# One mask a group, a new order in the recurrence with decays, and both ends of the program rewritten, in a two-layer hybrid block

## The reference, cut to what matters

```python
def rmsnorm(x, g):
    xf = x.astype(jnp.float32)
    y = xf * lax.rsqrt(jnp.mean(xf * xf, -1, keepdims=True) + EPS)
    return (y * g).astype(x.dtype)

# in ssd_group, for each group g with its E = 4 heads:
cb = jnp.einsum('bclgn,bcsgn->bgcls', Cm, Bm)              # one matrix a group
y_diag = jnp.einsum('bgecls,bcsgep->bclgep', cb[:, :, None] * jnp.exp(segsum(a_dt)), X)   # four decays a group
...
return rmsnorm(h, final_norm)[:, N_META:]
```

## Time and profile before

| | |
|---|---|
| runs, median (lowest to highest) | 1816.45 us (1816.36 to 1817.53) |
| the profiled execution, its own time | 1813.89 us |
| its span, first to last instruction | 1812.0 us |
| busy: TensorE / VectorE / ScalarE / GpSimd | 1770.1 / 1205.4 / 729.5 / 50.1 us |
| TensorE's mean granted clock | 0.995 of full |

### The profile page before, as it was taken

How to read it: one execution, slowest core, us unless ns; L and a number is a source line. 1 busy time by engine, 2 the same in 40 slices (tenths; PEclk the granted TensorE clock), 3 DMA queues, 4 the chain that set the end, 5 groups by cost and what they waited for, 6 DMA issues and landing times.

```text
span 1812.0 us, 35225 instructions
## 1 busy us (share of the span) xinstructions
PE 1770.1 (98%) x13934; PEld 1685.2 (93%) x13934; DVE 1205.4 (67%) x1702; ACT 729.5 (40%) x1074; POOL 50.1 (3%) x130
## 2 busy tenths in 40 slices
PE   7999999999999999999999999999999999999996
PEld 7988888999999999999999888888889999999996
DVE  7788846446367778874334777777776788888323
ACT  5454431112134233222223777777774322223221
POOL 0221200000000000000000000000000000000000
PEclk9999999999999999999999999999999999999998
DMA  4322232221222222322222212112123222223221
GB/s 154 109 77 86 94 107 61 80 70 58 70 83 92 92 83 91 93 91 95 96 74 81 62 62 62 57 53 61 59 59 93 83 92 93 93 93 99 92 96 62
DMA packets 39936, 149.89 MB, mean 83 GB/s; under 512 B 4384, under 2 KB 5408, under 8 KB 39216
## 3 DMA queue, kind: packets, MB, share of 16 engines
q1 hardware_dynamic: 38672, 142.16, 24.6%
q10 hardware_dynamic: 1184, 6.60, 1.1%
HBM read 146.62 MB, written 2.13 MB: 82 GB/s over the span
## 4 chain that ended last, share of the span: by engine, by line
PE 82%; issue 8%; DVE 6%; ACT 3%; POOL 1%; DMA 0%; DVEq 0%; ACTq 0%; POOLq 0%
PE gp L365 70%; PE small L411 4%; PE small L422 1%; PE small L605 1%; PE small L615 1%; DVE wlo L1112 1%; POOL dec L1734 1%; DVE spb L1563 1%; PE small L464 1%; DVE gr L1152 1%; ACT lbuf L959 1%; ACT lbuf L962 0%; DVE sp_lo L1587 0%; DMA rdec<-in 0%; ACT whi L698 0%
## 5 line engine op out<-in xcount | busy, mean ns | idle before, releaser
L365 PE MATMUL gp<-hn_hi,whi 128*128 128x264 f32 (+1 forms) x3216 | 661.6, 287 | 15.3 <-DVE wlo L1112 11.8
L365 PE MATMUL gp<-hn_hi,wlo 128*128 128x264 f32 (+1 forms) x3216 | 653.4, 285 | 0.0
L365 PE MATMUL gp<-hn_lo,whi 128*128 128x264 f32 (+1 forms) x3216 | 653.2, 284 | 0.0
L698 ACT ACTIVATE whi<-raw 128x1024 fp32r<-128x1024 f32 (+1 forms) x249 | 273.6, 1099 | 796.0 <-PE gp L365 785.9
L1112 DVE TENSOR_TENSOR wlo<-raw,whi 128x1024 fp32r<-128x1024 f32 (+1 forms) x249 | 317.5, 1275 | 345.6 <-ACT whi L698 337.5
L365 PEld LDWEIGHTS gp<-hn_hi,whi 128*128 128x128 f32 x3216 | 501.8, 189 | 20.5 <-DVE wlo L1112 14.2
L365 PEld LDWEIGHTS gp<-hn_lo,whi 128*128 128x128 f32 x3216 | 500.0, 189 | 0.0
L365 PEld LDWEIGHTS gp<-hn_hi,wlo 128*128 128x128 f32 x3216 | 498.8, 189 | 0.0
L365 PE MATMUL gp<-hid_lo,whi 128*128 128x264 f32 (+1 forms) x704 | 141.5, 282 | 0.0
L365 PE MATMUL gp<-hid_hi,whi 128*128 128x264 f32 (+1 forms) x704 | 141.2, 282 | 0.0
L365 PE MATMUL gp<-hid_hi,wlo 128*128 128x264 f32 (+1 forms) x704 | 141.2, 282 | 0.0
(11 more groups left out here) (233 smaller groups left out, 1763.7 us busy)
## 6 DMA issues: line engine op xcount, KB each, us to landing
raw<-in SPq DMA_DIRECT2D x217, 512.0 KB, 3.5
raw<-in SPq DMA_DIRECT2D x32, 704.0 KB, 4.0
cs_bc<-cs_scratch ACTq DMA_DIRECT2D x4, 1056.0 KB, 7.0
hT<-in SPq DMA_DIRECT2D x4, 528.0 KB, 7.5
out<-yT SPq DMA_DIRECT2D x4, 512.0 KB, 2.8
rdec<-in ACTq DMA_DIRECT2D x1, 1056.0 KB, 7.4
gw<-in SPq DMA_DIRECT2D x8, 128.0 KB, 3.4
rope<-in ACTq DMA_DIRECT2D x1, 528.0 KB, 4.2
```

What stands on the lines that cost most here:

```text
L365: ins = pe.matmul(gp[t.par][:, h, 0:half], wp[w.par][:, cols], rp[:, k0 + k, t0 + h * half:t0 + (h + 1) * half], start=first and k == 0 an ...
L698: act.activation(whi[w.par][:, 0:kt * P], raw[w.par][:, 0:kt * P], ACT.Copy).then_inc(hi_done, 1)
```

## The change: what it does

- **Start.** Unit 0 goes into banks 2 and 3 of `small`; a memset gives gp[0] free at once. ScalarE and VectorE do all eight `gained` first, then the split of unit 1, then the eight squares and sums; `sum_squares(0)` is done inside unit 1, behind its k-step 6. ScalarE runs one root on a column ahead of everything, so that this table is loaded.
- **Mask.** GpSimd masks `cbs` once a group instead of `dec` four times; `weigh_pair` waits for `cbm_done` and the exponentials.
- **Orders in a stage.** VectorE: `args` 0 and 1 ahead of the split in slot 0, `weigh_pair` 0 in slot 2, `args` 2 and 3 and `conv_` 2 in slot 3, `conv_` 3 in slot 4. ScalarE: silu of B, z, x, C in this order, decays 2 and 3 in step 4, the log of g-2 ahead of the split and its exponential behind it.
- **Tables.** `rope` and `rdec` lie elsewhere and are loaded in step 5 once the last SSD values are done; before, they waited for `yout_done`.
- **End.** Sums of squares per token: four matmuls against one column of ones on `acc` and four on the last tile's squares, root and reciprocal on 128x4, and four matmuls that spread the result over the partitions. The gain is put on hT by ScalarE tile by tile; VectorE multiplies hT and PSUM (128x512), eight stores of one tile each.

```diff
...
         nsp, nspt = sb("nsp", [P, 8]), sb("nspt", [P, 8])
+        frs = sb("frs", [P, 4])
         idle_g, idle_v, idle_a = (sb(n, [P, 6]) for n in ("idle_g", "idle_v", "idle_a"))
...
             with scope() as s2:
-                rope = sb("rope", [P, 2, T], f32, s2)
-                rdec = sb("rdec", [P, RET_HEADS, T], f32, s2)
                 rq = sb("rq", [P, 2, T], f32, s2)
...
                 o_tok = sb("o_tok", [P, NT, 256], f32, s2)
+                rope = sb("rope", [P, 2, T], f32, s2)
+                rdec = sb("rdec", [P, RET_HEADS, T], f32, s2)
                 stats = sb("stats", [P, NT, 6], f32, s2)
...
-            for c in range(KD // 2):
-                sp.wait_ge(final_done, 2 * c + 2)
-                sp.dma_start(out[:, 2 * c:2 * c + 2, :], yT[:, 2 * c:2 * c + 2, N_META:T]).then_inc(out_done, 16)
-            sp.wait_ge(out_done, 16 * (KD // 2))
+            for c in range(KD):
+                sp.wait_ge(final_done, c + 1)
+                sp.dma_start(out[:, c, :], yT[:, c, N_META:T]).then_inc(out_done, 16)
+            sp.wait_ge(out_done, 16 * KD)
...
             def gemm(w, t, rhs_hi, rhs_lo, k0=0, kt=KD, first=True, last=True, ready=None, after=None, t0=0,
-                     freed=None):
+                     freed=None, psum=None):
                 half = (T - t0) // 2
+                psum = gp[t.par] if psum is None else psum
...
                         for h in range(2):
-                            ins = pe.matmul(gp[t.par][:, h, 0:half], wp[w.par][:, cols],
+                            ins = pe.matmul(psum[:, h, 0:half], wp[w.par][:, cols],
                                             rp[:, k0 + k, t0 + h * half:t0 + (h + 1) * half],
...
-            hgemm(At(0, 0, W_DT), At(0, 0, T_DT), ready=(nlo_done, 0))
-            pe.wait_ge(const_in, 16)
-            sum_squares(0)
+            gemm(At(0, 0, W_DT), At(0, 0, T_DT), hn_hi, hn_lo, ready=(nlo_done, 0), psum=sp_[:, 2:4, :])
+
+            def norm_first(k):
+                if k == 6:
+                    pe.wait_ge(const_in, 16)
+                    sum_squares(0)
             for c in range(6):
-                hgemm(At(6, 0, W_SSD + c), At(6, 0, T_SSD + c))
+                hgemm(At(6, 0, W_SSD + c), At(6, 0, T_SSD + c), after=norm_first if c == 0 else None)
                 if c == 2:
...
             project(W_FO1, T_FO1, hid_hi, hid_lo, KH, (hlo_done, KF), t0=FROM_OUT)
-            sum_squares(4)
+
+            def token_sums(src, first=False, last=False):
+
+                for i in range(4):
+                    at = N_META + P * i
+                    ins = pe.matmul(sp_[:, 0, i:i + 1], src[:, at:at + P], ones[:, 0:1], start=first and i == 0,
+                                    stop=last, skip_group_check=True)
+                if last:
+                    ins.then_inc(fsum_done, 1)
+
+            pe.wait_ge(acc_done, 5 * KD - 1)
+            token_sums(acc, first=True)
+            pe.wait_ge(sq_done, 5 * KD)
+            token_sums(sq[:, 1, :], last=True)
+            pe.wait_ge(finv_done, 1)
+            for i in range(4):
+                ins = pe.matmul(sp_[:, 1, P * i:P * (i + 1)], frs[:, i:i + 1].to_broadcast([P, P]), ident, start=True,
+                                stop=True)
+            ins.then_inc(fbc_done, 1)
...
             act.dma_start(cst[:], cst_h[:, 0:5 * P]).then_inc(const_in, 16)
+            act.wait_ge(prep_done, 1)
+            act.activation(idle_a[:, 1:2], eps_col[:], ACT.Sqrt)
             act.wait_ge(vec_in, 16)
...
                     split_hi(At(0, 0, 0))
+            split_hi(At(0, 0, 1))
+            for m in range(KD):
                 square(0, m, m % 2)
-            split_hi(At(0, 0, 1))
             split_hi(At(6, 0, W_SSD + 1))
-            act.wait_ge(prep_done, 1)
             root(0)
...
-                act.wait_ge(conv_done, 4 * (g + 1))
-                act.activation(xcv[:, 2:4, :], xcv[:, 2:4, :], ACT.Silu)
+                act.wait_ge(conv_done, 4 * g + 3)
+                act.activation(xcv[:, 2, :], xcv[:, 2, :], ACT.Silu)
+                act.wait_ge(pair_free[(T_SSD + 4) % 2], (T_SSD + 4) // 2 + 1 + 3 * g)
+                act.activation(zc[:, 0, :], zc[:, 0, :], ACT.Silu)
                 wait_count(act, ysum_done, g)
                 act.activation(xs[:], xcv[:, 0:2, :], ACT.Silu)
-                act.wait_ge(pair_free[(T_SSD + 4) % 2], (T_SSD + 4) // 2 + 1 + 3 * g)
-                act.activation(zc[:, 0, :], zc[:, 0, :], ACT.Silu)
+                act.wait_ge(conv_done, 4 * g + 4)
+                act.activation(xcv[:, 3, :], xcv[:, 3, :], ACT.Silu)
...
                     act.activation(cbs[0:SZ[4], FULL:CAUSAL], sp_[0:SZ[4], 2, 416:432], ACT.Copy).then_inc(cbs_done, 1)
-                if step == 3:
+                if step == 4:
                     for h in range(2, 4):
...
                     ins.then_inc(yln_done, 1)
+                if step == 7:
                     act.wait_ge(yln_done, g + 1)
...
                 for c in range(6):
+                    back = c == 0 and not (isinstance(g, int) and g < 2)
                     if c == 0:
                         ssd_small(g - 1, 0)
+                    if back:
+                        ssd_small(g - 2, 6)
                     split_hi(At(6, g, W_SSD + c + 1))
+                    if back:
+                        ssd_small(g - 2, 7)
                     if c > 0:
                         ssd_small(g - 1, c)
-                    if c == 0 and not (isinstance(g, int) and g < 2):
-                        ssd_small(g - 2, 6)
                     if c == 4:
...
             for c in range(8):
+                back = {0: SSD_GROUPS - 2, 6: SSD_GROUPS - 1}
                 if c == 0:
                     ssd_small(SSD_GROUPS - 1, 0)
+                if c in back:
+                    ssd_small(back[c], 6)
                 split_hi(At(8, 0, W_RET + c + 1))
+                if c in back:
+                    ssd_small(back[c], 7)
                 if 0 < c < 6:
                     ssd_small(SSD_GROUPS - 1, c)
-                if c in (0, 6):
-                    ssd_small({0: SSD_GROUPS - 2, 6: SSD_GROUPS - 1}[c], 6)
-                if c == 7:
-
-                    act.wait_ge(yout_done, SSD_GROUPS)
+                if c == 5:
+
+                    act.wait_ge(y_done, 2 * SSD_GROUPS)
                     act.dma_start(rope[:], cst_h[:, 5 * P:5 * P + 2 * T].rearrange("p (a t) -> p a t", a=2))\
...
                         split_hi(At(4, i, wb + 2 * s + 3), kt)
+                    if last and not following:
+                        act.activation(idle_a[:, 1:2], eps_col[:], ACT.Sqrt)
                     t = At(2, i, tb + s)
...
                         gained(n, m)
+                    else:
+                        act.wait_ge(sq_done, KD * n + m + 1)
+                        act.activation(hT[:, m, N_META:T], hT[:, m, N_META:T], ACT.Copy,
+                                       scale=pcol(NORMS[n], m)).then_inc(fgain_done, 1)
...
             project(W_FO1, T_FO1, KH, 4, following=False)
-            root(4)
+            act.wait_ge(fsum_done, 1)
+            act.activation(frs[:], sp_[:, 0, 0:4], ACT.Sqrt, scale=1.0 / D_MODEL,
+                           bias=eps_col[:, 0:1]).then_inc(froot_done, 1)
...
                 ve.memset(ub[:, s, 0:3], 0.0)
-            ve.memset(one_row, 1.0)
+            ve.memset(one_row, 1.0).then_inc(pair_free[0], 1)
             ve.memset(eps_col[:], EPS).then_inc(prep_done, 1)
...
                     split_lo(At(0, 0, 0))
+            split_lo(At(0, 0, 1))
+            for m in range(KD):
                 add_squares(0, m, m % 2, first=m == 0)
-            split_lo(At(0, 0, 1))
             ve.wait_ge(const_in, 16)
...
             ve.wait_ge(unit_done, 1)
-            ve.tensor_tensor(halves(dtx), gp[0][0:16, :, 0:H2], halves(rstd[0:16, :]),
-                             ALU.mult).then_inc(pair_free[0], 1)
-            ve.wait_ge(pair_free[0], 1)
+            ve.tensor_tensor(halves(dtx), sp_[0:16, 2:4, 0:H2], halves(rstd[0:16, :]),
+                             ALU.mult).then_inc(dtx0_done, 1)
+            ve.wait_ge(dtx0_done, 1)
             ve.tensor_scalar(dtx, dtx, pcol("ssd_dtb", rows=16), None, ALU.add).then_inc(dtx_done, 1)
...
                 for h in (2 * c, 2 * c + 1):
-                    ve.wait_ge(es_done, HPG * g + h + 1)
-                    ve.wait_ge(cbs_done, g + 1)
+                    ve.wait_ge(e_done, HPG * g + h + 1)
+                    ve.wait_ge(cbm_done, g + 1)
                     e = dec[h]
...
                     tile(-1)
-                    split_lo(w)
                     args(g, 0)
                     args(g, 1)
+                    split_lo(w)
                 elif c == 1:
...
                     conv_(1)
+                    weigh_pair(g, 0)
+                elif c == 3:
+                    split_lo(w)
+                    tile(2)
                     args(g, 2)
                     args(g, 3)
-                elif c == 3:
```

(31 more changed lines are left out.)

## The result

The changed kernel takes 1801.57 us in the median (1801.41 to 1804.47) against 1816.99 before, measured beside it (15.4 us less): a ratio of 0.9919, 95% interval 0.9901 to 0.9936, which is faster by 14.7 us (11.6 to 18.0). Two later series with five runs of the changed kernel each give medians 13.5 and 13.8 us apart. Forecast: 1804.2, from 1798.5 to 1810.5.

The account below looks back on a forecast made before the run. TensorE, busy for 98% of the 1812.0 us span, was taken to bound the kernel. Gains of 0.6 + 0.7 + 3.0 + 3.6 + 4.3 = 12.2 us off 1816.45 gave 1804.2, range 1798.5 to 1810.5.

Parts of the forecast that it names:

- the likeliest case: Whole kernel: the forecast of 1804.2 us itself, chance 0.47, own range 1802.2 to 1806.5.
- I carry it over: Whole kernel: the 12.2 us gain, reckoned on the profiled execution (1813.89), is subtracted from the median 1816.45.
- the first rival: SSD stages and start: nothing is late in the stages, 16.5 us gained, 1800.0 us; chance 0.19.
- The rival of the clock: Start and loop: the clock falls at new waits, 1.5 us each, 5 less gain, 1809.5 us; chance 0.13.
- Start: Program start: reciprocal at 24.4, unit 4 at 39.5 instead of 40.13; gain 0.6 us, bounds 0 to 2.2.
- Stages: SSD stages: fewer waits for the logarithm; gain 0.7 us in the first stage, 3.0 in two loop passes.
- The ring: SSD loop: tile 4's read, TensorE's k-steps and sums, ScalarE's chain back to VectorE's split; 47.6 us a pass, before 48.95.
- Mask: SSD stages: the one mask left, 1.2 to 3.4 us, fits before conv_ 1 ends and is hidden.
- The prediction's rival: SSD stages: VectorE holds the mask back until conv_ 1 ends, 1.4 us a pass, 3.3 less gain, 1807.5; chance 0.12.
- Tables: First rotations of the retention: earlier table loads remove waits of 1.7 and 2.2 us; gain 3.6 us.
- the 0.3 taken off: Tables: deduction of 0.3 us (0 to 1.5) because their 1.5 MB meet the load of unit 7's raw.
- End: Program end: products begin at 1799.5, not 1803.23, and stores set the end; gain 4.3 us (3.5 to 5.3).

Follow-up runs that it names:

- e2_after: The changed kernel unaltered, run again as base of the second series: 1801.51 us, ratio 0.9924 to the kernel before.
- e3_after: The changed kernel unaltered, run again as base of the third series: 1801.75 us, ratio 0.9924 to the kernel before.
- e1: First series: one part of the change at a time on the kernel before, whose own 25 runs beside it took 1815.42 us.
- e1_end: The kernel before with the edits of the end alone: 1812.80 us, ratio 0.9986 to the kernel before.
- e2_mask4: The changed kernel with GpSimd's four masks a group on the decays again, orders kept: 1807.45 us, 5.9 above the changed kernel.
- e2_conv: The changed kernel with conv 2 back in slot 4 and conv 3 behind tile 4 in slot 5: 1800.00 us, 1.5 under the changed kernel.
- e3_root: The changed kernel without the early root at the very start: 1803.84 us, 2.1 above the changed kernel.
- e1_start: The kernel before with the edits of the start alone: 1815.00 us, ratio 1.0000 to the kernel before.
- e1_stages: The kernel before with the mask and the orders of the SSD stages alone: 1809.23 us, ratio 0.9966 to the kernel before.
- e1_tables: The kernel before with only the two retention tables moved and loaded earlier: 1809.98 us, ratio 0.9973 to the kernel before.

## Why the prediction came out

**What bounds, and the sum.** The forecast time was 2.6 us too high; the time is inside the stated range and 0.6 below the likeliest case's own (1802.2 to 1806.5). Held against profiles, the sum was right: the one of before has a span of 1812.0, and its only fall of the clock cost nothing, as shown above; those of e2_after and e3_after, which have none inside the work, have 1799.5 and 1799.8. That is 12.2 to 12.5 us against 12.2. It is partly luck. In e2_after the start gives 0.3 (0.6 predicted) and the end 3.3 (4.3), the first stage 0.8 (0.7), the loop 3.8 (3.0) and the rotations 4.3 (3.6): the misses cancel.

The step to correct is the last: "I carry it over". The profiled execution of before (1813.89) was one of its faster ones, and the few runs that the forecast started from were on the slow side: their median of 1816.45, and the 1816.99 beside the result, lie 1.0 and 1.6 above the median of the 25 runs beside e1. These 25 runs of before lie between 1813.1 and 1818.1 us, 13 of the changed kernel's 14 between 1801.1 and 1801.9; the fourteenth is the profiled 1804.47, whose span is 3.2 longer than e2_after's and whose two falls cost 1.5 and 1.6. Of the 14 profiles of this study, that of before and the one of each later kernel counted, seven have no fall inside the work, and in the seven others each of the ten falls lies directly behind a wait of TensorE: at 160 (2.2 us, before), 208 (2.2, e1_end), 193 (1.9, e2_mask4), 41 to 43 (1.5, three kernels), and at 993 to 1004 (1.8 us in layer 1, which no edit touches, four kernels). The row of e1_end with its window:

```profile
207.98 2.10 PE L397 MATMUL small<-cst,xs 128*128 128x128 f32 x10 [2.24 <-ACT acc L800]
```

```profile
208.00:212.00 4.00, 4.00 (x21) 3.85 (x22) 2.99 (x9) 3.96 (x4) 0.00 (x0) 0.57 0.38 123
```

Such a wait doesn't always bring a fall: the wait ahead of 993 is in every profile (it ends between 988 and 1002). The kernel before has four waits of 1.4 to 2.2 us that the change removes, the changed kernel one of 1.5 that it adds. Between the fastest runs of both (1813.1 and 1801.1) there are 12.0 us, between their medians 13.5 to 15.4. That the difference is what the falls give back is argued, not shown; the timed runs show a mean clock (0.994 to 0.996 before; 0.997 in 13 of 14 after, 0.995 in the slow one), not where it fell. The clock does go with the time: of the 43 runs of before beside the experiments, the 18 at 0.994 take 1816.7 us in the mean and the others 1814.4.

The measured 1801.6 lies nearer to the first rival's 1800.0 than to the forecast, but that rival did not come true: the new waits are there, 1.7 us of them in the two passes. The rival of the clock came true in part: behind the new wait of 1.5 us ahead of unit 4 it fell in the profiled execution, in e2_conv and in e3_root, and not in e2_after and e3_after.

**Start**, 0.6 predicted: reciprocal at 24.4 (24.8 measured), unit 4 at 39.5 (39.8), gain 0.4; e1_start measured none. The same start varies: the reciprocal begins between 24.6 and 25.6 in the six profiles that have all of it. That the load's removal gains nothing at the first matmul was right; that the same load is worth 1.3 us ahead of the root (e3_root) was in the chain but not told.

**Stages**, 0.7 and 3.0 predicted, 0.8 and 3.8 measured: L394's successor at 109.1 (109.06 in e2_after, which has no fall there), passes of 47.2 and 47.6 (46.8 and 47.3). TensorE alone needs 45.8, not 46.1 (e2_conv). The ring was right, including that tile 4 and decays 2 and 3 are late next; TensorE waits 1.7 us in both passes together, not in each; which of the ring's terms was too long the runs don't separate. e2_conv shows the cause of what is left: the new places of `conv_` 2 and 3 cost 2.5 us, so this part of the change was a loss. e1_stages shows the sum (6.2 by the ratio, 4.7 at the loop's end in its profile). Which of the other orders removed the waits for the logarithm no run tells apart.

**Mask**: hidden, as taken. GpSimd is done at 124.0 in the loop's first pass, VectorE weighs 1.7 us later. By the rule of the Trainium skill (GPSIMD Engine Reference, Specifications), that GpSimd and VectorE contend for SBUF when VectorE has two SBUF inputs, masks should be slower beside convolutions. The traces agree: five blocks took 1.17 us with VectorE idle, 1.83 here and 3.15 in e2_mask4. Taken block by block it is more than a slowing. The last block of that mask, 16x16, takes 0.19 us when nothing disturbs it; here it ends with VectorE's split:

```profile
137.69 1.31 DVE L1156 TENSOR_TENSOR wlo<-raw,whi 128x1024 fp32r<-128x1024 f32 x1
137.88 1.17 POOL L1782 TENSOR_SCALAR_AFFINE_SELECT dec<-dec 16x16 f32<-16x16 f32 x1
```

In the profiles of before, after and e2_mask4 all 38 blocks of these masks that take over 0.4 us end 0.05 to 0.16 us after an instruction of VectorE that reads SBUF alone (31 of them one with two SBUF inputs, 7 the convolution's first, which has one). The prediction's rival was thus right in kind and wrong in size: a mask waits for the end of one such instruction, not of the whole `conv_`, and gets a block through in the gaps of 0.15 us between its four.

**Tables**, 3.6 predicted: 4.3 in the profile (the waits are 3.9 of it), 4.9 by e1_tables. `raw` of unit 7 landed in 6.2 us instead of 3.5 and was in time; the 0.3 taken off was not due.

**End**, 4.3 predicted, 3.3 in the profile, 2.5 (0.9 to 4.2) by e1_end's ratio. From the last unit to the first product I had 3.9 us and it took 5.2: the sums of the last tile took 1.05 for 0.75 and the spreading 2.08 for "1.05 to 1.6"; hand-overs are the rest. From the first product to the end it was 7.9 for 8.1: the stores flow at the same rate as in the earlier trace rows. But the 3.3 compares two ends with the clock falling at different places. In before it fell at 1798.7, behind most of the norm's sums; in the changed kernel at 1792.3, ahead of the spreading. Where it falls early in the old end too (e1_start, at 1797) that end takes 17.2 us against the new one's 13.1; where it falls late in both it is 16.4 (before) against 12.3 (e1_end): 4.1 either way, to 0.1. So the term was near, and what it left out is that the moment of the fall moves either end by 0.8 us.

## What to carry to other kernels

Where one engine is full and the next at 95% of the same time, an order that moves work ahead of a read-out moves the wait, not the work: name the read-out that frees a buffer, and put nothing in front of it that isn't needed for it. A norm's chain is longer than the matmuls that it no longer delays; starting the first unit's successor early bought nothing while the reciprocal got later. Price a wait of TensorE of one and a half to two microseconds above its length where TensorE sets the pace, since it may also bring a stretch at half clock; where another engine sets the pace, as in the loop before, the stretch can cost nothing. Compare medians of several runs for the time, and for the cause two profiles in which the clock fell at the same places.

## What was not expected of the hardware

A stretch at 1.2 GHz cost some 1.5 us where TensorE set the pace (41 to 43 and 993 to 1004 us), 0.7 and 1.1 where a later wait took up a part (e2_mask4 at 193, e1_end at 208), and nothing at 160 in before. It came, in some executions and not in others, behind waits of TensorE of 1.5 to 2.2 us; the 25 runs of the kernel with four such waits that the edits touch scatter by 5 us, 13 of 14 of the changed one by 0.8, the last 2.6 above them. At the end of the program the moment of the fall relative to the last matmuls changes their time between 1.16 and 2.08 us (ten profiles). A small mask on GpSimd that takes 0.19 us alone took 1.17 because VectorE's split was under way. And the tables' 1.5 MB beside a 512 KB load slowed that load from 3.5 to 6.2 us, less than the 8 that I had reckoned.
